# Level 0 of the RWKV inversion moved by a product instead of ten turns, with the vector load behind four tiles of x and smaller first and last output pieces

## What is computed

```
h = RMSNorm(x); P = h @ w_in
A: mLSTM, 8 heads x 128     B: HGRN2, 4 heads x 128     C: RWKV-7, 8 heads x 64
merged = sum_b sigmoid(gate_b) * (y_b @ w_proj_b)
x' = x + RMSNorm(merged @ w_out)
```

```
sa    = S @ (-kk)
S_new = S * w + sa (kk*a)^T + v k^T
y     = S_new @ r
```

## Time and profile before

| | |
|---|---|
| three runs | 2222.31, 2222.31, 2222.06 us (median 2222.31) |
| the profiled execution, its time | 2221.52 us |
| its span in the profile | 2219.7 us, so 1.8 us lie outside the span |
| PE busy | 2186.7 us, 99% of the span |
| DVE busy | 1347.9 us, 61% |
| ACT busy | 788.0 us, 36% |
| POOL busy | 63.8 us, 3% |
| DMA | 249.33 MB, 112 GB/s over the span |

### The profile page before, as it was taken

The page is one execution under the profiler, slowest core; times in us unless marked ns, Lnnn a source line. Parts: engine busy times, 40 slices in busy tenths (PEclk is TensorE's granted clock), DMA queues, the critical chain, the costliest instruction groups (busy, mean ns, idle before and its releaser), DMA issues.

```text
span 2219.7 us, 44655 instructions
## 1 busy us (share of the span) xinstructions
PE 2186.7 (99%) x18901; PEld 2151.0 (97%) x18901; DVE 1347.9 (61%) x2105; ACT 788.0 (36%) x1209; POOL 63.8 (3%) x93
## 2 busy tenths in 40 slices
PE   6999999999999999999999999999999999999997
PEld 5999999999999999999999999999999999999997
DVE  5444444488777777676657484755777755454354
ACT  5321221234333333333334242424333443244443
POOL 0000001000000000000000000000000000000000
PEclk9999999999999999999999999999999999999999
DMA  5422222233333333334112121204111353434465
GB/s 184 134 79 97 84 86 90 76 106 119 121 135 110 120 120 124 126 119 169 59 52 83 42 74 45 88 22 151 67 67 67 112 207 139 163 138 171 151 216 181
DMA packets 67352, 249.33 MB, mean 112 GB/s; under 512 B 9082, under 2 KB 16428, under 8 KB 50612
## 3 DMA queue, kind: packets, MB, share of 16 engines
q1 hardware_dynamic: 67204, 247.14, 32.1%
HBM read 216.92 MB, written 30.19 MB: 111 GB/s over the span
## 4 chain that ended last, share of the span: by engine, by line
PE 98%; DMA 1%; DVE 0%; SPq 0%; ACT 0%; issue 0%; DVEq 0%; POOL 0%; ACTq 0%; POOLq 0%
PE acc L1009 52%; PE acc L1198 16%; PE branch L1198 8%; PE acc L1608 7%; PE branch L1608 2%; PE branch L1297 1%; PE branch L1497 1%; PE branch L1313 1%; PE branch L1322 1%; DMA scratch<-in_x_all 1%; PE acc L1052 1%; PE branch L1287 0%; PE branch L1365 0%; PE branch L1628 0%; PE branch L1144 0%; PE branch L1137 0%
## 5 line engine op out<-in xcount | busy, mean ns | idle before, releaser
L1009 PE MATMUL acc<-act_hi,w_hi 128*128 128x320 f32 (+3 forms) x2848 | 869.0, 305 | 0.0
L1009 PE MATMUL acc<-act_lo,w_hi 128*128 128x320 f32 (+3 forms) x2848 | 845.4, 297 | 0.0
L1009 PE MATMUL acc<-act_hi,w_lo 128*128 128x320 f32 (+3 forms) x2848 | 845.4, 297 | 0.0
L1009 PEld LDWEIGHTS acc<-act_hi,w_hi 128*128 128x128 f32 x2848 | 537.3, 189 | 11.0 <-issue 5.0
L1009 PEld LDWEIGHTS acc<-act_lo,w_hi 128*128 128x128 f32 x2848 | 537.2, 189 | 0.7
L1009 PEld LDWEIGHTS acc<-act_hi,w_lo 128*128 128x128 f32 x2848 | 537.0, 189 | 0.0
L2149 DVE TENSOR_TENSOR w_lo<-w_raw,w_hi 128x2048 fp32r<-128x2048 f32 x119 | 272.5, 2290 | 228.1 <-ACT w_hi L1666 225.6
L1666 ACT ACTIVATE w_hi<-w_raw 128x2048 fp32r<-128x2048 f32 x120 | 229.8, 1915 | 132.9 <-PE branch L1608 125.7
L1198 PE MATMUL acc<-corner_terms,w_hi 128*128 128x288 f32 x768 | 154.5, 296 | 0.0
L1198 PE MATMUL acc<-act_hi,w_hi 128*128 128x288 f32 x512 | 151.6, 296 | 0.0
L1198 PE MATMUL acc<-act_lo,w_hi 128*128 128x288 f32 x512 | 151.4, 296 | 0.0
(11 more groups left out here) (470 smaller groups left out, 3502.9 us busy)
## 6 DMA issues: line engine op xcount, KB each, us to landing
w_raw<-in_w_stream SPq DMA_DIRECT2D x122, 1024.0 KB, 4.8
w_raw<-in_w_stream SPq DMA_DIRECT2D x96, 512.0 KB, 5.9
gate_logits<-gate_out SPq DMA_DIRECT2D x48, 288.0 KB, 2.2
scratch<-gate_logits SPq DMA_DIRECT2D x48, 288.0 KB, 5.2
scratch<-in_x_all SPq DMA_DIRECT2D x9, 512.0 KB, 6.0
branch_rows<-branch_out SPq DMA_DIRECT2D x16, 288.0 KB, 2.2
scratch<-in_x_all SPq DMA_DIRECT2D x3, 1024.0 KB, 10.7
out_y_prompt<-scratch SPq DMA_DIRECT2D x6, 512.0 KB, 3.0
```

The source lines that it names most:

```text
L1009: last = mm(acc[s][:, at:at + hi - lo], a[:, s, w], b[:, k, lo:hi], start=(k == order[0] and a is whi and b is xh), stop=(k == order[-1] a ...
```

## The change

Five edits.

1. The level 0 inverse is not turned any more. DVE subtracts `UU` from `EE0` as before (now itself the step inv0, without the copy of a block). PE forms one f32 product of `UU` (128x320) with a shifted identity (`next_row`, the identity's columns begun one column early, for which two columns of zeros, `lead`, stand ahead of it in `full`). POOL fills `DD1` with unit blocks too, between its two operations on `EE0` and `DDT`. DVE subtracts the product from `DD1`, behind the mixing of v and ahead of the `w_lo`. ACT's five copies are gone. PE's `turn_first` waits for yk1 instead of inv0, and level 1 waits for this subtraction (turned_inv0) instead of ACT's t0.
2. The bonus sums move from block 31 to block 30.
3. SP loads the vectors behind tiles 0 to 3 of x, and the constants behind tile 1 instead of tile 0.
4. ACT and DVE wait for the vectors behind their five tiles instead of ahead of them.
5. Row tiles 3 and 4 are finished and stored in six pieces of 512, 512, 1024, 1024, 512, 512 columns instead of four of 1024.

```diff
-    full = {"ident": np.eye(P), "blocks": s // 64 == t // 64}
+    full = {"lead": np.zeros((P, 2)), "ident": np.eye(P), "blocks": s // 64 == t // 64}
...
+        next_row = full[:, CONST_AT["ident"][0] - 1:CONST_AT["ident"][1] - 1]
...
+        LAST_PIECES = [(3, (0, D // 4)), (3, (D // 4, D // 2)), (3, (D // 2, D)), (4, (0, D // 2)), (4, (D // 2, D // 4 * 3)), (4, (D // 4 * 3, D))]
...
         def _(sp):
-            sp.dma_start(vecs[:, :], vecs_in).then_inc(vecs_here, 16)
             for t in range(5):
                 for a, b, src in given(t, ROWS[t]):
                     sp.dma_start(xt[a:b, t, :], src).then_inc(x_here[t], 16)
-                if t == 0:
+                if t == 1:
                     sp.dma_start(full[:, :], full_in).then_inc(consts_here, 16)
+                elif t == 3:
+                    sp.dma_start(vecs[:, :], vecs_in).then_inc(vecs_here, 16)
...
-            for m in range(4):
+            for m in range(len(LAST_PIECES)):
                 sp.wait_ge(rows_done, 4 + m)
-                rows_out(3 + m // 2, m % 2)
+                last_rows_out(m)
...
                     if lv == 1:
-                        pe.wait_ge(*at.after(i, "t0"))
+                        pe.wait_ge(*vt.after(i, "turned_inv0"))
...
                 def turn_first():
-                    pe.wait_ge(*vt.after(i, "inv0"))
-                    turn_squares(EE0, 0)
+                    pe.wait_ge(*vt.after(i, "yk1"))
+                    pt.done(mm(brb[:, 0:320], next_row, UU[:, :, 0:32], start=True, stop=True), "turned0")
...
-                plan += [(31, bonus), (39, w1), (46, solved)]
+                plan += [(30, bonus), (39, w1), (46, solved)]
...
             S = S0["setup_scalar"]
-            act.wait_ge(vecs_here, 16)
...
+            act.wait_ge(vecs_here, 16)
             act.wait_ge(w_here[0], 16)
...
-                act.wait_ge(*G.after(i, "turned0"))
-                squares_out(lambda r, qs: DD1[r, qs, :], 0)
...
-            dve.wait_ge(vecs_here, 16)
             for t in range(5):
...
+            dve.wait_ge(vecs_here, 16)
             for k in range(KT):
...
-                tt(EE0[:, 0:10, 1::2], EE0[:, 0:10, 1::2], UU[:, :, 0:32], ALU.subtract, "inv0_part")
-                own("inv0_part")
-                V.done(v.tensor_copy(EE0[64:128, 10, :], EE0[64:128, 0, :]), "inv0")
+                tt(EE0[:, 0:10, 1::2], EE0[:, 0:10, 1::2], UU[:, :, 0:32], ALU.subtract, "inv0")
                 dve.wait_ge(evac_done, N(2) + 1)
                 mixed(cvv, PB[0], DD, pv[:, MU + 2:MU + 3], V, i, "v")
+                dve.wait_ge(*Q.after(i, "turned_unit_blocks"))
+                dve.wait_ge(*G.after(i, "turned0"))
+                tt(DD1[:, 0:10, 0::2], DD1[:, 0:10, 0::2], brb[:, 0:320].rearrange("p (q n) -> p q n", q=10), ALU.subtract, "turned_inv0")
                 split_lo(N(4))
...
                 dve.wait_ge(res_here[t], 16 * 2)
-                for h in range(2):
-                    finish(t, h * D // 2, h * D // 2 + D // 2)
+                for u, (a, b) in LAST_PIECES:
+                    if u == t:
+                        finish(t, a, b)
...
                 Q.done(g.tensor_tensor(EE0[:, 0:10, :], each, each, ALU.mult), "unit_blocks")
+                Q.done(g.tensor_tensor(DD1[:, 0:10, :], each, each, ALU.mult), "turned_unit_blocks")
                 Q.done(g.memset(DDT[:, :, :], 0.0), "square_zeros")
```

More of the change, by code:

```diff
@@ L295 @@
         k_factor k_new kk kkh b bE kE bh kh r_step r end_decays rh bonus_terms bu0 bu1 uk0 uk1 yb0 yb1 low0
-        yk0 yk1 inv0_part inv0 v_step v low1 inv1 low2 inv2 low3 inv3 bonus state0 low4 inv4 z_step z low5 inv5_part inv5
+        yk0 yk1 inv0 v_step v turned_inv0 low1 inv1 low2 inv2 low3 inv3 bonus state0 low4 inv4 z_step z low5 inv5_part inv5
         w1 z1 z2_part low6 z2 inv6 gate tv u0 state1 sample_state u1 state2 u2 state3 u3 state4 u4 state5
@@ L299 @@
     "rwkv_scalar": """
-        rank_exps decay_exps kk_squares kk_log kk_rsqrt kk_rows bE_rows kE_rows bonus_hi t0 v_rows
+        rank_exps decay_exps kk_squares kk_log kk_rsqrt kk_rows bE_rows kE_rows bonus_hi v_rows
         t1 t2 t3 t4 z_exp t5 tk out0 out1 out2 out3 out4
@@ L308 @@
     "rwkv_pool": """
-        unit_blocks square_zeros bonus_lo""",
+        unit_blocks turned_unit_blocks square_zeros bonus_lo""",
     "hgrn_vector": """
@@ L943, in half_cols, with last_rows_out @@
                 return slice(h * D // 2, h * D // 2 + D // 2)
+            def last_rows_out(m):
+                t, (h0, h1) = LAST_PIECES[m]
+                a, b = ROW_TILES[t][3:5]
+                for lo, hi, to in wanted_rows(a, b):
+                    sp.dma_start(to[:, h0:h1], YT[lo:hi, t, h0:h1]).then_inc(stored, 16)
             def old_rows(t, h):
@@ L980, in _ @@
                     rows_out(2, 1)
-            for m in range(4):
+            for m in range(len(LAST_PIECES)):
                 sp.wait_ge(rows_done, 4 + m)
-                rows_out(3 + m // 2, m % 2)
-            sp.wait_ge(stored, 16 * 2 * sum(len(wanted_rows(*ROW_TILES[t][3:5])) for t in range(5)))
+                last_rows_out(m)
+            early_stores = 2 * sum(len(wanted_rows(*ROW_TILES[t][3:5])) for t in range(3))
+            sp.wait_ge(stored, 16 * (early_stores + sum(len(wanted_rows(*ROW_TILES[t][3:5])) for t, _ in LAST_PIECES)))
             sp.wait_ge(shift_out, 32)
```

## The result

The changed kernel takes 2224.86 us, the median of 22 runs (2223.14 to 2227.92). The kernel before, run beside it as often, takes 2222.06 (2221.12 to 2223.47). The ratio is 1.0014, with a 95% interval of 1.0007 to 1.0020. So the change costs 2.8 us where 0.3 were forecast, and 2224.86 lies 0.8 above the upper end of the range. It is still within the 0.2% that the prediction had called no change.

A forecast was written before the change was run, and what follows sets the result against it. The prediction took PE's own work, busy 99% of the span, to bound the kernel. Its terms, +0.6 (new wait), -0.2 (start) and -0.1 (end), summed to +0.3, so 2222.6 us, with a range of 2218.6 to 2224.1.

The forecast's parts named there:

- Edits at nothing: ACT's copies, bonus sums, the `DDT` memset and two more columns of constants (1 KB): all claimed to cost nothing.
- PE, level 0: Level 0 of each RWKV round: one product replaces ten turns, block 1.36 us instead of 2.05, saving 0.69 a round.
- The new wait: Ahead of level 1: DVE, held behind POOL's reading operations, makes PE wait about 0.85 us; net 0.16 a round, +0.6 in all.
- rival 1: RWKV rounds: nothing stands in DVE's way, so no PE wait; -2.8 there, -3.1 in all, 2219.2 us; chance 0.26.
- The start: Loads at the kernel's start: x issued ahead of the vectors, so tile 4 lands 0.2 us earlier (0 to 0.45).
- the price inside the stream: Kernel start: the vectors' own transfer, still ahead of tile 4 in the DMA queue, takes 0.24 us off the 0.45 lead.
- The end: Last finishes and stores: smaller pieces start earlier but leave a hole in the stream; -0.1 us, between +0.2 and -0.6.
- The sum: Whole kernel: +0.6 for the middle, -0.2 for the start, -0.1 for the end, together +0.3 us; 2222.6 forecast.

The follow-up runs named there:

- the gap alone: The kernel before with 32 bytes of unused SBUF behind the constants and nothing else changed: median 2223.17 us, ratio 1.0005.
- the combination: The changed kernel with a gap of 8 floats behind `full`, POOL's other order and the four old last pieces: median 2218.26 us, ratio 0.9984.

## Why the prediction was wrong, step by step

**The step that failed** is the last sentence of "Edits at nothing": "Two more columns of constants are 1 KB." I priced the transfer and not the place. The two columns push `corner_terms` up by 32 bytes, and that costs +1.38 us in a stage that I had not looked at because the change does nothing there; the same shift gives 0.44 back in RWKV. Net it is +0.9, a third of the 2.8. Three runs show it from both sides: the gap alone brings it, 32 bytes taken back remove it, and 32 bytes more turn it into a gain. No step of my working had a term for it. Without it the measured time lies inside the range: the changed kernel with `corner_terms` at its old place is 1.1 above the kernel before beside it, which on the 2222.3 of the prediction is 2223.4.

**PE, level 0** was right: 1.36 us for the block, 0.69 saved. **The new wait** was right in place, size and cause: PE waits 0.77 (0.85 forecast), DVE is the releaser, the two long operations are the forecast ones. From the pair products (L1307, 1087.72) to level 1 it is now 7.79 us, 0.15 more than before, and 0.16 was forecast. Over the stage, against a kernel of the same place, it is +0.69 at +32, +0.58 at +64 and +0.43 at the old place, where +0.6 was forecast. There was luck in it: the choice hung on DVE coming 0.1 us behind bonus_lo, and it came 0.01 or less behind, in all four rounds. A layout worked out to some 0.1 us could not tell which of the two would be first. The run with POOL's other order shows what the cover was worth: without the two stops the same kernel gains 3.16, of which 0.44 are the place, so 2.7, and rival 1 had put nothing in the way at -2.8. The Trainium skill (SBUF — State Buffer, Who interferes with whom) says that an operation which started first holds the shared pair until it is done; the 1.39 and 1.54 agree with it, at starts 0.21 and 0.01 behind POOL's. The same section says that such a DVE operation contends only with a POOL operation that reads, and the 0.77 across a memset agrees. No run has DVE begin first.

**Edits at nothing, the rest.** ACT's copies, the bonus sums and the memset cost nothing that a row shows. But the wait that the change adds to DVE did more than wait. In every kernel DVE stands for over a microsecond once, in head 0 of HGRN, for nothing that the trace names. With the change's DVE code the stop comes one operation earlier and is longer (1.62 instead of 1.19), PE waits 0.3, and the stage costs +0.35 to +0.64 in five kernels with it and 0.10 at most in the others. Taking one wait out of DVE's code puts it back. I had no term for that either: +0.45 in the changed kernel.

**The start** had the right sign, and its size is not refuted: the term of -0.2 (0 to -0.45) measures -0.5 in the means of seven and seven profiles, with an uncertainty of about as much. The run of this part alone is 1.2 below the kernel before in the median, and its interval (-3.1 to +0.9) tells nothing about the size. Tile 0's square begins 0.65 earlier, where 0.45 for the issue of the vectors were counted. Tile 3's, with the load of the vectors no longer ahead of it, begins 0.86 earlier, and tile 4's, behind the vectors again, 0.52. That the lead shrinks by 0.34 there fits the price inside the stream that I had put at 0.24. But from tile 2 (0.58) to tile 3, with nothing new ahead of either, it grows by 0.28, so the price cannot be read to that size.

**The end** had the wrong sign: -0.1 (+0.2 to -0.6) measures +0.44 alone and +0.40 in the changed kernel. The hole came as forecast. The measured cost is twice my upper bound. What was mis-sized are the small pieces with rows of 2 KB and their two issues: I named them for that bound only, and the last two flow at 344 to 373 GB/s and cost 0.2, and the end of the span comes 0.2 later behind them.

**The sum**, with what was measured: level 0 +0.6, place +0.9, HGRN +0.45, start -0.5, end +0.4 make +1.9, and 2.8 (1.6 to 4.4 by the interval) were measured. The profiled execution, at +3.3, holds the late weight tile (+0.6) as well. From HGRN's head 0 to the end's first finish the kernels drift by up to 0.5 more beside late tiles. About half of that comes evenly between 2004 and 2120 us, where PE's list names no wait: +0.15 in the changed kernel, +0.22 to +0.24 in the four kernels at +64 and in the one with the old place, but 0.01 at most in the three kernels in which no tensor moved. So a place acts there too. It is not that of `corner_terms`, which lies where it lay in the kernel with the old place (+0.24); which tensor it is was not followed. The rest is a step of up to 0.17 near 2000 us (0.6 in the combination), only in kernels with the change's level 0; that is not explained.

One bound was also added up wrong: the range's lower limit takes -0.4 for the end of the kernel, where the paragraph on the end has -0.6. The miss is on the other side.

**Still open.** What the stop in HGRN is: that its place goes with DVE's code is shown by one run and fits all profiles. That DVE waits there for instructions to be loaded is argued from the packet ahead of it in all 14 profiles; no run tests it, the profile does not say for which engine a packet is, and the other 27 packets of that queue in the kernel before come without such a stop of DVE. Why `corner_terms` is fast at three places and slow at two is not known; the runs fit a period of 128 bytes (-64 and +64 agree) and show no more. That the scratch's place also moves RWKV by -0.24 to -0.44, whichever way it goes, was seen and not followed.

## What to carry to other kernels

When a change makes a tensor longer, list what lies behind it in SBUF. The products out of one operand got slower by 0.9% through a shift of 32 bytes up and faster by 0.6 to 0.8% through other shifts here, in a stage that nobody edited, so measure a padded twin of both kernels before you believe a difference of 0.1%. When PE loses an instruction and its successor's input comes from DVE, look for what POOL reads in those microseconds: moving two POOL operations here turned +0.7 into -2.7 at the same place. Smaller last pieces with rows of 2 KB cost 0.4 here; no other size was tried.

## What the runs showed of the hardware that was not expected

- The rate of these matmuls depends on where their moving operand lies. Two products of 24 matmuls of 288 columns out of `corner_terms`, at a granted clock of 0.998: 6.39 us at its old place, 6.45 at +32 bytes, 6.34 at +64, 6.35 at -32, 6.34 at -64. The other nine profiles agree with these to 0.01, each with that of its place.
- One wait more or less in DVE's code moves a stop of 1.2 to 1.8 us by one operation, in the next stage of the kernel. The stop ends 1.75 to 1.83 us after a packet of an instruction queue, in all 14 profiles.
- A DVE operation with both inputs in scratch that begins 0.01 us behind a reading one of POOL's (1092.74 against 1092.73) is held for nearly the whole of POOL's 1.47: it takes 1.54 instead of 0.28.
- The last stores of 512 columns (rows of 2 KB) flow at 355 GB/s, up to the end of their data, where those of 1024 columns ahead of them flow at 391 to 406.
